# Three key/value units of the first layer as seven half-block products each

## The reference, cut to what matters

```python
def memory_cross_attention(h, mem_n, wq, wkv, qn_g, kn_g, wo):
    ...
    k, v = jnp.split(mem_n @ wkv, 2, axis=-1)
    k = rmsnorm(k.reshape(B, MEM_LEN, XA_HEADS, XA_HEAD_DIM), kn_g)
    ...
for l in range(DEPTH):
    h = rmsnorm(x, norm1_g[l])
    ...
    x = x + mix @ w_out[l]
    h = rmsnorm(x, norm2_g[l])
    m = rmsnorm(mem, mem_norm_g[l])
    x = x + memory_cross_attention(h, m, ...)
    h = rmsnorm(x, norm3_g[l])
    x = x + hierarchical_moe(h, ...)
```

## Time and profile before

| what | value |
|---|---|
| time, median of 3 runs | 1399.17 us (1399.04 to 1399.39) |
| the profiled execution's own time | 1398.2 us |
| its span, first to last instruction | 1396.4 us |
| TensorE busy | 1155.2 us, 83% |
| VectorE busy | 326.6 us, 23% |
| ScalarE busy | 199.3 us, 14% |
| mean granted TensorE clock | 0.926 |
| chain that ended last | TensorE 48%, DMA 46% |

### The profile page before, as it was taken

How to read it: one execution, slowest core, us unless ns; L and a number is a source line. 1 busy time by engine, 2 the same in 40 slices (tenths; PEclk the granted TensorE clock), 3 DMA queues, 4 the chain that set the end, 5 groups by cost and what they waited for, 6 DMA issues and landing times.

```text
span 1396.4 us, 14663 instructions
## 1 busy us (share of the span) xinstructions
PE 1155.2 (83%) x6066; PEld 547.9 (39%) x6066; DVE 326.6 (23%) x849; ACT 199.3 (14%) x463; POOL 46.0 (3%) x87
## 2 busy tenths in 40 slices
PE   8999999997869686686769999999966757677578
PEld 5775455553323231222315786465312212122123
DVE  1216553132111110110102287233211101111011
ACT  3024412210101000000002252231000000000000
POOL 1111001000000000000000200100000000000000
PEclk9999999998989799888979999999988887879899
DMA  9563274389999999999998354546999999999998
GB/s 386 223 241 121 81 285 175 133 344 425 432 430 431 430 428 433 429 431 431 429 431 367 125 181 159 223 189 228 428 431 429 432 429 429 432 429 431 430 431 339
DMA packets 36453, 478.00 MB, mean 342 GB/s; under 512 B 4422, under 2 KB 5406, under 8 KB 6558
## 3 DMA queue, kind: packets, MB, share of 16 engines
q1 hardware_dynamic: 35319, 475.12, 81.9%
q10 hardware_dynamic: 1063, 1.87, 0.4%
HBM read 475.93 MB, written 1.05 MB: 342 GB/s over the span
## 4 chain that ended last, share of the span: by engine, by line
PE 48%; DMA 46%; DVE 4%; issue 1%; ACT 1%; POOL 0%; DVEq 0%; SPq 0%; ACTq 0%; POOLq 0%
PE bank L1565 46%; DMA ring<-experts 45%; PE bank L1572 2%; DMA X<-x 0%; DVE X L1147 0%; DVE fox_ssd L1309 0%; DVE proj_ht L1136 0%; DVE Y L1400 0%; DVE Y L1395 0%; DVE keys_values L1065 0%; DVE proj_ht L1060 0%; DVE dqt_sco L1399 0%; ACT proj_ht L830 0%; DVE dqt_sco L1302 0%; ACT H L986 0%
## 5 line engine op out<-in xcount | busy, mean ns | idle before, releaser
L1565 PE MATMUL bank<-ring,proj_ht 128*32 128x512 f32 (+4 forms) x3424 | 573.6, 658 | 188.1 <-DMA ring<-experts 177.8
L1565 PEld LDWEIGHTS bank<-ring,proj_ht 128*32 128x32 f32 (+1 forms) x3424 | 184.2, 130 | 515.1 <-DMA ring<-experts 253.3
L1147 DVE TENSOR_TENSOR X<-X,bank 128x512 f32<-128x512 f32 (+1 forms) x66 | 44.3, 672 | 307.1 <-PE bank L1565 307.1
L1565 PE MATMUL bank<-ring,H 128*128 128x512 f32 x256 | 112.5, 593 | 0.0
L1565 PE MATMUL bank<-proj_ht,H 128*128 128x128 f32 x512 | 74.0, 296 | 23.1 <-DVE proj_ht L1091 16.7
L1565 PEld LDWEIGHTS bank<-proj_ht,H 128*128 128x128 f32 x512 | 64.9, 202 | 60.1 <-issue 33.3
L1136 DVE SCALAR_TENSOR_TENSOR proj_ht<-Y,bank 128x512 f32<-128x512 f32 x16 | 17.1, 1066 | 257.4 <-PE bank L1565 257.4
L1565 PEld LDWEIGHTS bank<-ring,H 128*128 128x128 f32 x256 | 48.0, 190 | 55.8 <-issue 55.0
L1565 PE MATMUL bank<-fox_ssd,proj_ht 128*128 128x512 f32 (+3 forms) x180 | 64.9, 564 | 2.1 <-ACT proj_ht L830 1.4
L1565 PE MATMUL bank<-ahead,conv_mem 128*128 128x512 f32 x128 | 60.2, 626 | 1.8 <-DVE keys_values L1065 1.8
L1565 PE MATMUL bank<-ring,conv_mem 128*128 128x512 f32 x128 | 56.5, 594 | 0.0
(11 more groups left out here) (214 smaller groups left out, 782.6 us busy)
## 6 DMA issues: line engine op xcount, KB each, us to landing
ring<-experts SPq DMA_DIRECT2D x177, 2048.0 KB, 25.4
ring<-dense SPq DMA_DIRECT2D x24, 2048.0 KB, 8.3
ahead<-dense SPq DMA_DIRECT2D x4, 2048.0 KB, 23.9
ring<-dense SPq DMA_DIRECT2D x6, 1024.0 KB, 18.4
ahead<-experts SPq DMA_DIRECT2D x3, 2048.0 KB, 12.7
conv_mem<-experts SPq DMA_DIRECT2D x3, 2048.0 KB, 17.4
fox_ssd<-experts SPq DMA_DIRECT2D x2, 2048.0 KB, 9.9
keys_values<-experts SPq DMA_DIRECT2D x2, 2048.0 KB, 7.8
```

Of the source, the lines that this page charges most:

```text
L1147: v.tensor_tensor(x, x, bank[b][:, 0:w], ALU.add).then_inc(s.x_added, 1)
L1565: return nc.tensor.matmul(dst, lhsT, rhs, start=start, stop=stop)
```

## The change

Units 0, 2 and 1 of the first layer, in this order, are computed by a scheme of seven products of half blocks. The memory is cut into four blocks (two halves of rows, two halves of the contraction), each unit into four (two halves of the contraction, two halves of columns). A product is then 4 matmuls of 128 x 128 by 128 x 256. VectorE forms four sums of memory blocks once (`sum_memory`) and four sums of weight blocks for each unit (`sum_weights`, `sum_last_weights`), and adds the products into the result (`sum_first`, `sum_second`); ScalarE copies two products out of their banks (`copy_first`) and applies the norm's scale later, from the buffer (`scale_sums`). Unit 3 stays as it was. The list `BETWEEN` is written anew: a unit's three first products stand in one round, the other four in the next. The jobs `kx` are new and take banks of their own.

```diff
-BETWEEN = [[[("kv", 0, 0)], [("kv", 0, 1)], [("dT", 0), ("dT", 1), ("kT", 0, 0), ("kv", 1, 0)],
-            [("kT", 0, 1), ("kv", 1, 1)], [("kT", 1, 0), ("kv", 2, 0)], [("kT", 1, 1), ("kv", 2, 1)],
-            [("kv", 3, 0)], [], []],
+KV_FAST = (0, 2, 1)
+BETWEEN = [[[("kv", 0, 0)], [("kv", 0, 1)], [("dT", 0), ("dT", 1), ("kv", 2, 0)], [("kv", 2, 1)],
+            [("kT", 0, 0), ("kT", 0, 1), ("kv", 1, 0)], [("kv", 1, 1)], [("kv", 3, 0)], [],
+            [("kT", 1, 0), ("kT", 1, 1)]],
...
+            def sum_weights(i):
+
+                w = dense_arrived(dve, 0, ("kv", KV_FAST[i]))
+                if i:
+                    dve.wait_ge(*full(0, ("kv", KV_FAST[i - 1], 1)))
+                v.tensor_tensor(W_SUM[0], weights(w, 0, 1), weights(w, 0, 0), ALU.subtract).then_inc(W_summed, 1)
+                dve.wait_ge(W_summed, 4 * i + 1)
+                v.tensor_tensor(W_SUM[1], weights(w, 1, 1), W_SUM[0], ALU.subtract).then_inc(W_summed, 1)
+                v.tensor_tensor(weights(w, 0, 1), weights(w, 1, 1), weights(w, 0, 1), ALU.subtract).then_inc(W_summed, 1)
+                dve.wait_ge(W_summed, 4 * i + 3)
+
+            def sum_last_weights(n):
+
+                i = KV_FAST.index(n)
+                w = dense_arrived(dve, 0, ("kv", n))
+                dve.wait_ge(*full(0, ("kv", n, 0)))
+                v.tensor_tensor(weights(w, 1, 0), weights(w, 1, 0), W_SUM[1], ALU.subtract).then_inc(W_summed, 1)
+
+            def sum_first(n):
+
+                i, job = KV_FAST.index(n), ("kv", n, 0)
+                dve.wait_ge(*full(0, job))
+                dve.wait_ge(p1_copied, i + 1)
+                v.tensor_tensor(kv_part(n, 0, 0), kv_part(n, 1, 0), bk(0, job)[:, S:2 * S], ALU.add
+                                ).then_inc(read(0, job), 1)
+
+            def sum_second(n):
+
+                c00, c01, c10, c11 = [kv_part(n, t, j) for t in range(NT) for j in range(2)]
+                job, last = ("kx", n, 1), ("kv", n, 1)
+                b, b_last = bk(0, job), bk(0, last)
+                dve.wait_ge(*full(0, job))
+                dve.wait_ge(*copied(0, ("kv", n, 0)))
+                link(v.tensor_tensor(c10, c10, b[:, S:2 * S], ALU.add))
+                v.tensor_tensor(c11, c10, b[:, 0:S], ALU.add).then_inc(read(0, job), 1)
+                dve.wait_ge(*copied(0, job))
+                dve.wait_ge(*copied(0, ("kx", n, 0)))
+                link(v.tensor_tensor(c01, c01, c11, ALU.add))
+                dve.wait_ge(*full(0, last))
+                v.tensor_tensor(c11, c11, b_last[:, 0:S], ALU.add)
+                link(v.tensor_tensor(c10, c10, b_last[:, 0:S], ALU.add))
+                v.tensor_tensor(c10, c10, b_last[:, S:2 * S], ALU.add).then_inc(read(0, last), 1)
+                dve.wait_ge(*copied(0, last))
+                dve.sem_inc(kv_summed, 1)
...
                 if l == 0:
                     gain_memT(0)
+                    sum_memory()
+                    sum_weights(0)
...
                     if k < len(HEADS):
                         mask_scores(k)
+                        for job in BETWEEN[l][k]:
+                            if by_sevens(l, job) and job[2] == 1:
+                                sum_last_weights(job[1])
                         conv(k)
...
-                        if job[0] == "kv" and job[1] < 2:
-                            norm_k(l, *job[1:])
+                        if by_sevens(l, job):
+                            (sum_first, sum_second)[job[2]](job[1])
+                            if job[2] == 1 and KV_FAST.index(job[1]) + 1 < len(KV_FAST):
+                                sum_weights(KV_FAST.index(job[1]) + 1)
+                    for job in BETWEEN[l][k - 2] if k >= 2 else ():
+                        if by_sevens(l, job) and job[1] < 2 and job[2] == 1:
+                            for t in range(NT):
+                                norm_k(l, job[1], t)
...
+                def kv_sevenths(n, part):
...
+                    if part == 0:
+                        pe.wait_ge(MT_ready, 1)
+                        job, then = ("kv", n, 0), ("kx", n, 0)
+                        pe.wait_ge(*free(0, job))
+                        seventh(bk(0, job)[:, 0:S], memory(0, 0), weights(w, 0, 0))
+                        seventh(bk(0, job)[:, S:2 * S], memory(0, 1), weights(w, 1, 0)).then_inc(filled(0, job), 1)
+                        pe.wait_ge(M_summed, 4)
+                        pe.wait_ge(*free(0, then))
+                        seventh(bk(0, then)[:, 0:S], M_SUM[3], weights(w, 1, 1)).then_inc(filled(0, then), 1)
+                    else:
+                        job, then = ("kx", n, 1), ("kv", n, 1)
+                        pe.wait_ge(*free(0, job))
+                        pe.wait_ge(W_summed, sums + 1)
+                        seventh(bk(0, job)[:, 0:S], M_SUM[0], W_SUM[0])
+                        pe.wait_ge(W_summed, sums + 2)
+                        seventh(bk(0, job)[:, S:2 * S], M_SUM[1], W_SUM[1]).then_inc(filled(0, job), 1)
+                        pe.wait_ge(*free(0, then))
+                        pe.wait_ge(W_summed, sums + 3)
+                        seventh(bk(0, then)[:, 0:S], M_SUM[2], weights(w, 0, 1))
+                        pe.wait_ge(W_summed, sums + 4)
+                        seventh(bk(0, then)[:, S:2 * S], memory(1, 1), weights(w, 1, 0)).then_inc(filled(0, then), 1)
```

More of the change, by code:

```diff
@@ L130, in score_jobs, with by_sevens, with_halves @@
     return [("s", head, t) for t in range(NT) for head in heads]
+def by_sevens(l, job):
+    return l == 0 and job[0] == "kv" and job[1] in KV_FAST
+def with_halves(l, jobs):
+    for job in jobs:
+        if not by_sevens(l, job):
+            yield job
+        elif job[2] == 0:
+            yield from (job, ("kx", job[1], 0))
+        else:
+            yield from (("kx", job[1], 1), job)
 def list_jobs(l):
@@ L343, in trunk, with memory, weights, kv_part @@
         K_tm = (XS, view(fox_ssd, 0, NT, 512))
+        HW = KC // 2
+        M_SUM = [view(ahead, i * HW * P, HW, P) for i in range(4)]
+        W_SUM = [view(ahead, UNIT // 2 + i * HW * S, HW, S) for i in range(2)]
+        def memory(t, k):
+            return MT_all[:, k * HW:(k + 1) * HW, t * P:(t + 1) * P]
+        def weights(w, k, j):
+            return w[:, k * HW:(k + 1) * HW, j * S:(j + 1) * S]
+        def kv_part(n, t, j):
+            if n < 2:
+                return K_tm[0][:, t, j * S:(j + 1) * S]
+            return VM[:, t, (n - 2) * 512 + j * S:(n - 2) * 512 + (j + 1) * S]
         dqt_flat = DQT[:, :, :].rearrange("p a b -> p (a b)")
@@ L818, in take_kv, with copy_first, scale_sums @@
                     act.wait_ge(k_ss, at(k_ss, l, NT * n + t + 1))
+            def copy_first(n):
+                if n == 1:
+                    for t in range(NT):
+                        act.wait_ge(*full(0, ("kT", 0, t)))
+                act.wait_ge(*full(0, ("kv", n, 0)))
+                nc.scalar.copy(kv_part(n, 1, 0), bk(0, ("kv", n, 0))[:, 0:S]).then_inc(p1_copied, 1)
+                job = ("kx", n, 0)
+                copy_out(0, job, kv_part(n, 0, 1), bk(0, job)[:, 0:S])
+            def scale_sums(n):
+                act.wait_ge(mem_rs, 1)
+                act.wait_ge(kv_summed, KV_FAST.index(n) + 1)
+                for t in range(NT):
+                    both = K_tm[0][:, t, :] if n < 2 else VM[:, t, (n - 2) * 512:(n - 1) * 512]
+                    last = nc.scalar.activation(both, both, ACT.Copy, scale=ss[:, t:t + 1])
+                    if n < 2:
+                        link(last)
+                        for h in range(2):
+                            part = slice(h * XD, (h + 1) * XD)
+                            last = nc.scalar.activation(k_junk[0][:, part], K_tm[0][:, t, part], ACT.Square,
+                                                        accum_out=ssk[:, t, 2 * n + h:2 * n + h + 1])
+                        last.then_inc(k_ss, 1)
+                if n >= 2:
+                    last.then_inc(v_scaled, 1)
             def quad(l, q, n, s):
@@ L1880, in kv, with seventh @@
                     tile_job(l, ("kv", n, t), arrived(l, ("kv", n)), t, MT)
+                def seventh(dst, a, b):
+                    for c in range(HW):
+                        last = mm(dst, a[:, c, :], b[:, c, :], start=c == 0, stop=c == HW - 1)
+                    return last
+                def kv_sevenths(n, part):
+                    i, w = KV_FAST.index(n), arrived(0, ("kv", n))
+                    sums = 4 * i
+                    if part == 0:
[7 more added lines that the diff above has]
+                        seventh(bk(0, then)[:, 0:S], M_SUM[3], weights(w, 1, 1)).then_inc(filled(0, then), 1)
+                    else:
+                        job, then = ("kx", n, 1), ("kv", n, 1)
[9 more added lines that the diff above has]
+                        seventh(bk(0, then)[:, S:2 * S], memory(1, 1), weights(w, 1, 0)).then_inc(filled(0, then), 1)
                 def attend(k):
```

54 lines of the change are left out of this document (38 added, 16 removed).

## The result

The changed kernel takes **1410.79 us** (median of 6 runs, 1409.68 to 1412.39), the kernel before 1399.28 us beside it (6 runs, 1397.79 to 1401.02): a ratio of 1.0083, 95% interval 1.0073 to 1.0094. It is slower by 11.5 us; forecast were 1410 us, range 1405 to 1415. The profiled execution took 1411.2 us with a span of 1409.4, 13.0 more than before.

The account below looks back on a forecast made before the run. TensorE bounds the rounds (busy 65.94 of 68 us). Stalls 13.7 less 0.8 and 4.6 make 8.3 us; with 2.8 of clock on 1398.2, 1409.3, plus 1.0 to the median: 1410 us, range 1405 to 1415.

Parts of the forecast that it names:

- Products: TensorE's seven half-block products, 256-column instructions 0.218 us apart: 1.55 us saved a unit, 4.6 us in all.
- Stalls: TensorE's new waits in rounds 2 to 8, mostly for banks or norms from VectorE: 13.7 us in sum.
- banks 2, 3 and 7, freed behind masks, convolution, gate and adds: Rounds 4 and 6: TensorE waits until VectorE's late adds free these banks; stalls 4.5, 1.3 and 3.3 us.
- The clock: TensorE's clock falls behind the stalls of rounds 4 and 6: 1.4 us added for each, 2.8 in all.
- One for one to the end: Behind the rounds: expert loads wait for TensorE, so every shift of the rounds passes whole to the end.
- Banks free in time: Rival for the rounds: the stalls do not arise, the change gives 4.6 + 0.8 us, 1394 us; chance 0.03.
- VectorE sets the pace: Rival for the rounds: weight sums take twice 1.14 us, VectorE lags some 9 us more, 1419 us; chance 0.07.
- The experts take it up: Rival behind the rounds: the experts' 85.2 us of DMA waits swallow the shift, 1399 us; chance 0.04.
- weight loads not hidden: Rival for TensorE's products: 0.41 us per 256-column instruction, 23 us a unit, 1440 us; chance 0.01.
- the clock stays full: Rival for the rounds: the stalls come without a clock drop, 1407 us, inside the range; chance 0.15.

Follow-up runs that it names:

- e1: Changed kernel with other bank numbers for 17 jobs of rounds 4 to 7, every engine's order kept: 1402.57 us, ratio 1.0019.
- e2: Changed kernel with VectorE doing `sum_second` ahead of the masks of its round: 1404.26 us, ratio 1.0030.
- e9: Changed kernel with the first three weight sums of units 2 and 1 made by VectorE before the rounds: 1411.79 us, ratio 1.0086.
- e5: Changed kernel with idle TensorE products (9, 1, 8 and 3) filling the stalls before unit 0's transposes, unit 3's job and unit 1's transposes: 1408.86 us, ratio 1.0063.
- e4: Changed kernel with weight sums of 256 columns, not 1024: rounds 79.8 us; its time, 1936.8 us, says nothing, since other keys bring more expert loads.
- e11: e10 with VectorE doing unit 1's `sum_second` ahead of round 6's masks and unit 1's norms at that round's end: 1395.22 us, ratio 0.9972.
- e10: e9's early weight sums together with e1's bank numbers, on the changed kernel: 1399.85 us, ratio 1.0004.
- e6: Changed kernel with the nine weight sums of the rounds on GpSimd in place of VectorE: 1424.55 us, ratio 1.0180.
- e8: e6 with e1's banks, and unit 1's `sum_second` ahead of round 6's masks, its norms at that round's end: 1410.52 us, ratio 1.0080.

## Why the prediction was right

The mechanism is the one predicted, place by place; two sizes were off, in opposite directions, and half cancel. Against the profile of before the sum gave 11.1 us (8.3 and 2.8 of clock), measured are 13.0. That 1410 us comes within 1 us of the median is in part luck: of the two profiled executions the one before lay 1.1 us under the median of its six runs and the one after 0.4 above, so the medians differ by 11.5 us only.

- **Products.** Unit 0's took 12.1 us (96.84 to 102.02 and 102.67 to 109.58) where 13.74 stood before: 1.65 saved a unit, forecast 1.55. The spacing of 0.216 us also decides what was weighed there against the Trainium skill ("TensorE: Matmul & The Clock Gate", section "Back-to-back issue gap"): half the columns take half the time here.
- **Stalls.** Round 2 1.5 (forecast 1.4); round 4 4.1 and 0.6 (4.5 and 1.3); round 5 0.6 (0.8); round 6 3.6 (3.3); rounds 7 and 8 1.5 (2.2); round 3 shows 0.2 between two of its products, as forecast. 12.1 in all, 13.7 forecast. In round 4 VectorE freed the bank when I had it (133.0, forecast 133.1); TensorE came 0.5 us later than I had it, at 129.07, and the transpose, slowed to 1.09 us, used up part of the second wait.
- **The cause of the stalls.** e1 removes the waits by bank numbers alone, e2 most of them by order, e9 only 0.5 us of them by 7.3 us less work. The step "banks 2, 3 and 7, freed behind masks, convolution, gate and adds" is shown.
- **The clock** is the term that was mis-sized: 2.8 forecast for two drops. There were three: the clock fell behind the 1.5 us of round 8 too, though the 1.5 of round 2 had left it at 1.00. Round 8's comes soon after the 1.2 before `attend`, which may be why; no run shows it. And a drop slowed more than the product behind it. By rows: transposes 0.5 each, product 1.6, unit 3's job 1.6, transposes and products of round 8 0.9 each, 6.0 in all. With the stalls filled (e5) 4.9 came back. Some 0.9 of the 6.0 lie where TensorE would have waited anyhow: behind a fast first transpose the wait for bank 3 is 1.1, not 0.6 (e4), and the transposes of round 8 take 1.45 at the full clock of e5, not 1.04.
- **Balance.** Stalls 12.1 less 0.8, clock 6.0, products 4.95 less: 12.3 of 13.0; the other 0.7 lie in pieces that I did not assign. Stalls were 1.6 too long in the forecast and the clock 3.2 too short; by e5's 4.9 it is 0.7 and 2.1.
- **One for one to the end.** The stretch behind the rounds is as long in all the kernels but e4 and e5 (1231.6 to 1233.4 us), at rounds from 63.9 to 92.9: the experts take up nothing, and give nothing.
- **The rivals.** "Banks free in time" was wrong for the kernel as it stands. With the banks free, six sums made early and round 6 in another order (e11) the time is 3.7 us under the kernel before (1395.22 against 1398.91 beside it), most of the 5.4 that this rival counts on. "VectorE sets the pace" needed sums of twice 1.14 us; they took 1.23, and e9 shows that less of this work does not remove the waits. "The experts take it up" fell with the 1232.6 us behind the rounds, "weight loads not hidden" with the 0.216 us, "the clock stays full" with the 0.53.

## What to carry to other kernels

Before work is moved to an engine with free time, look at where in that engine's order it will stand and who owns what it frees: here VectorE's 26 free microseconds did not hide the work, because the banks came free behind three other jobs, in a rotation that brought them round too early. Such waits can be moved by a table of buffer numbers or by order; making sums early, where the engine waits anyway, helped only once the banks came free in time (e9, e10). A wait of the matmul engine costs its own length and, behind most of the longer ones here, a slower clock as well (4.9 us beside 12.1 of waiting).

## What the runs showed of the hardware

- **GpSimd stops VectorE.** While one GpSimd operation on two operands in SBUF ran (2.35 us), VectorE's operations that read two SBUF operands lasted as long (2.25 to 2.38 in place of 0.22 us), and between two of GpSimd's only one came through (0.21 at 112.16). The Trainium skill ("SBUF — State Buffer", section "SBUF: two separate sides") says that the two engines share a pair of ports, that an operation holds for its whole length; the rows agree. A division of probabilities, with one large operand, lasted as well (2.29 us at 134.50 in e6, in place of 0.29). I had not weighed any of it before e6.
- **Pauses and the clock.** The 1.5 us of round 2 left the clock at 1.00 (97 to 128 us in e1 and e2). So did 2.3 and 2.1 us in e8 (136 to 168 us). Behind the 2.4 of e1 it fell (0.72 from 156 to 168 us), as behind the longer ones; and it fell behind the 1.5 of round 8 in the changed kernel, e2 and e9. So the length of a single pause does not tell whether it falls; what does stays open here. What a fall costs differs: behind the same wait of 3.59 us unit 3's job lost 1.6 us in the changed kernel (8.61) and 3.1 in e9 (10.10).
